# Two of eight tiles of a LayerNorm moved from VectorE to GpSimd and ScalarE, in a two-layer decoder step

## What is computed

```python
def layer_norm(x, g, b):
    xc = x - jnp.mean(x, -1, keepdims=True)
    var = jnp.mean(xc * xc, -1, keepdims=True)
    return xc * lax.rsqrt(var + LN_EPS) * g + b

for l in range(2):
    h = layer_norm(ALPHA * h + 0.5 * swiglu(h, ...), ln_g[l, 0], ln_b[l, 0])   # norms 0 and 3
    m = ab_mixer(h, ...) if l == 0 else gdn_mixer(h, ...)                      # RWKV-7 and retention; gated DeltaNet
    h = layer_norm(ALPHA * h + m, ln_g[l, 1], ln_b[l, 1])                      # norms 1 and 4
    h = layer_norm(ALPHA * h + 0.5 * swiglu(h, ...), ln_g[l, 2], ln_b[l, 2])   # norms 2 and 5
```

## Time and profile before

| | us |
|---|---|
| median of three runs | 1461.27 |
| lowest, highest run | 1460.04, 1465.32 |
| the profiled execution, whole | 1460.42 |
| its span, first to last instruction | 1458.6 |
| TensorE busy in it | 1393.0 (95%) |
| VectorE, ScalarE, GpSimd busy | 895.3 (61%), 648.1 (44%), 456.6 (31%) |

### The profile page before, as it was taken

How to read it: one execution, slowest core, us unless ns; L and a number is a source line. 1 busy time by engine, 2 the same in 40 slices (tenths; PEclk the granted TensorE clock), 3 DMA queues, 4 the chain that set the end, 5 groups by cost and what they waited for, 6 DMA issues and landing times.

```text
span 1458.6 us, 30569 instructions
## 1 busy us (share of the span) xinstructions
PE 1393.0 (95%) x12058; PEld 1325.9 (91%) x12058; DVE 895.3 (61%) x1194; ACT 648.1 (44%) x990; POOL 456.6 (31%) x478
## 2 busy tenths in 40 slices
PE   7999999887999999999999999999998899999996
PEld 7999999776979799999999999988987778999996
DVE  4444456776564565554677775568777467565554
ACT  4333336634234354333444443377683445333333
POOL 3333133542324212125312127431017551221343
PEclk9999999999999999999999999999999999999999
DMA  7555543310333355555445555434433125555541
GB/s 286 159 164 177 179 143 103 102 46 21 110 101 131 110 166 162 168 169 179 143 131 163 168 169 179 143 96 145 129 115 144 31 79 182 161 169 159 182 159 53
DMA packets 50767, 203.39 MB, mean 139 GB/s; under 512 B 5712, under 2 KB 5840, under 8 KB 49904
## 3 DMA queue, kind: packets, MB, share of 16 engines
q1 hardware_dynamic: 46368, 181.03, 38.8%
q0 software_dynamic: 4016, 19.81, 3.7%
q10 hardware_dynamic: 288, 1.18, 0.2%
HBM read 192.17 MB, written 9.83 MB: 138 GB/s over the span
## 4 chain that ended last, share of the span: by engine, by line
PE 83%; DVE 8%; ACT 4%; issue 3%; POOL 1%; DMA 0%; ACTq 0%; POOLq 0%; DVEq 0%
PE gemm L2661 23%; PE gemm L2665 23%; PE gemm L2662 23%; ACT whi L2593 2%; DVE wlo L2598 2%; DVE r L3114 1%; PE job L1790 1%; DVE rstd L3080 1%; PE job L892 1%; PE job L1729 0%; PE job L566 0%; PE job L2670 0%; POOL xsum L3212 0%; PE job L910 0%; DVE M L2323 0%
## 5 line engine op out<-in xcount | busy, mean ns | idle before, releaser
L2661 PE MATMUL gemm<-xhi,whi 128*128 128x290 f32 (+1 forms) x2032 | 615.0, 303 | 21.5 <-DVE wlo L2598 18.6
L2593 ACT ACTIVATE whi<-raw 128x1024 fp32r<-128x1024 f32 (+1 forms) x319 | 358.4, 1124 | 600.2 <-PE gemm L2665 596.5
L2598 DVE TENSOR_TENSOR wlo<-raw,whi 128x1024 fp32r<-128x1024 f32 (+1 forms) x319 | 433.7, 1360 | 301.9 <-ACT whi L2593 299.4
L2665 PE MATMUL gemm<-xlo,whi 128*128 128x290 f32 (+1 forms) x2032 | 606.5, 298 | 3.4 <-DVE xlo L3120 1.6
L2662 PE MATMUL gemm<-xhi,wlo 128*128 128x290 f32 (+1 forms) x2032 | 603.1, 297 | 0.0
L2661 PEld LDWEIGHTS gemm<-xhi,whi 128*128 128x128 f32 x2032 | 385.0, 189 | 35.4 <-DVE wlo L2598 21.2
L2665 PEld LDWEIGHTS gemm<-xlo,whi 128*128 128x128 f32 x2032 | 385.1, 190 | 5.8 <-DVE xlo L3120 2.3
L2662 PEld LDWEIGHTS gemm<-xhi,wlo 128*128 128x128 f32 x2032 | 385.8, 190 | 1.7
L2661 PE MATMUL gemm<-hhi,whi 128*128 128x288 f32 x704 | 209.7, 298 | 2.6 <-POOL hlo L3228 1.9
L2662 PE MATMUL gemm<-hhi,wlo 128*128 128x288 f32 x704 | 210.3, 299 | 0.0
L2665 PE MATMUL gemm<-hlo,whi 128*128 128x288 f32 x704 | 209.2, 297 | 0.0
(11 more groups left out here) (451 smaller groups left out, 1476.5 us busy)
## 6 DMA issues: line engine op xcount, KB each, us to landing
raw<-in_w_dram SPq DMA_DIRECT2D x255, 512.0 KB, 3.5
raw<-in_w_dram SPq DMA_DIRECT2D x64, 704.0 KB, 4.1
M<-in_ret_in_dram POOLq DMA_DIRECT2D x1, 2048.0 KB, 12.6
out_ret_s_dram<-M POOLq DMA_DIRECT2D x1, 2048.0 KB, 8.1
s_space<-in_gdn_in_dram POOLq DMA_DIRECT2D x4, 512.0 KB, 5.8
M<-in_gdn_in_dram POOLq DMA_DIRECT2D x4, 512.0 KB, 5.8
out_gdn_s_dram<-s_space POOLq DMA_DIRECT2D x4, 512.0 KB, 5.0
out_gdn_s_dram<-M POOLq DMA_DIRECT2D x4, 512.0 KB, 6.7
```

The costliest lines, as they stand in the source:

```text
L2593: nc.scalar.activation(whi[c % SPL][:, 0:w], raw[c % RAW][:, 0:w], ACT.Copy).then_inc(hi_ready, 1)
L2598: nc.vector.tensor_tensor(wlo[c % SPL][:, 0:w], raw[c % RAW][:, 0:w], whi[c % SPL][:, 0:w].bitcast(F32), ALU.subtract).then_inc(lo_ready, 1)
L2661: pe.matmul(bank[:, 0:w_], whi[s][:, w], hi[:, f0 + q, 0:w_], start=first, stop=False)
L2665: mm = pe.matmul(bank[:, 0:w_], whi[s][:, w], lo[:, f0 + q, 0:w_], start=False, stop=last)
```

## The change

VectorE scales tiles 0 to 5 and forms their low parts; tiles 6 and 7 are taken from it. GpSimd multiplies these two by rstd in place (`scale_tiles`), in norm 0 behind `a_mu1` and ahead of the wait for `shift_in`, in norm 3 behind the clearing of columns and ahead of the wait for `conv_in`, in norm 5 right behind `sum_tiles`. ScalarE applies ln_g as scale and ln_b as bias for the two, writes xhi and x of tile 6, xhi and x of tile 7, and then x of tiles 0 to 5. GpSimd forms their low parts as x - xhi (`low_tiles`), behind the copies `shift_pad` and `conv_pad`. A new semaphore, `pool_tiles`, counts GpSimd's four steps of a norm (two in norm 5): ScalarE waits for the first two, TensorE (`low_part_in`) for the others; the counts of `scaled` and `x_lo` are adapted.

```diff
--- before.py
+++ after.py
@@ -402,6 +402,20 @@
                 eng.wait_ge(sem("early"), (DT - 1) * EARLY[n] + d + 1)
             else:
                 eng.wait_ge(bank_free[2], TABLE[NORM_STAGE[n]][3][2] + DT // 2)
+
+        def lows_before(version):
+
+            return DT // 2 * version - sum(X_VERSION[n] < version for n in (0, 3))
+
+        def tiles_done(n):
+            return (0, 3, 5).index(n)
+
+        def low_part_in(pe, version, q):
+            for n in (0, 3):
+                if X_VERSION[n] == version and q >= DT - 2:
+                    pe.wait_ge(sem("pool_tiles"), 4 * tiles_done(n) + q - DT + 5)
+                    return
+            pe.wait_ge(x_lo[q % 2], lows_before(version) + q // 2 + 1)
 
         def wait_count(eng, s, count):
             if not isinstance(count, int) or count > 0:
@@ -1486,9 +1500,11 @@
             at = PCOLS["mu"][0]
             pool.wait_ge(sem("const_in"), 64)
             G.tensor_scalar(a_mu1, par[:, at:at + ZA], -1.0, 1.0, ALU.mult, ALU.add)
+            env["scale_tiles"](0)
             pool.wait_ge(sem("shift_in"), 16)
             G.tensor_copy(a_zp[:, :, 1 + SEQ:ZPW].rearrange("p t (b s) -> p t b s", s=5)[:, :, :, 0], a_sh
                           ).then_inc(sem("shift_pad"), 1)
+            env["low_tiles"](0)
 
             at = PCOLS["ka"][0]
             link(G.tensor_scalar(a_km, par[:, at:at + 4], 1.0, None, ALU.subtract))
@@ -2408,9 +2424,11 @@
             stage_read(pool, "down2")
             pool.dma_start(g_cin, a["conv_in"]).then_inc(sem("conv_in"), 16)
             G.memset(g_raw[:, :, 0:3], 0.0)
+            env["scale_tiles"](3)
             pool.wait_ge(sem("conv_in"), 16)
             G.tensor_copy(g_raw[:, :, 3 + SEQ:PADW].rearrange("p k (b s) -> p k b s", s=7)[:, :, :, 0:3],
                           g_cin).then_inc(sem("conv_pad"), 1)
+            env["low_tiles"](3)
             pool.wait_ge(sem("soft"), 1)
             link(G.tensor_scalar(rows_g, rows_g, 0.0, None, ALU.max))
             link(G.tensor_tensor(rows_g, rows_g, rows_e, ALU.add))
@@ -2620,7 +2638,7 @@
                     pe.wait_ge(x_hi, DT * version + q + 1)
                     pe.matmul(gemm[j][:, 0:T], whi[s][:, w], xhi[:, q, :], start=q == 0, stop=False)
                     pe.matmul(gemm[j][:, 0:T], wlo[s][:, w], xhi[:, q, :], start=False, stop=False)
-                    pe.wait_ge(x_lo[q % 2], DT // 2 * version + q // 2 + 1)
+                    low_part_in(pe, version, q)
                     pe.matmul(gemm[j][:, 0:T], whi[s][:, w], xlo[:, q, :], start=False, stop=False)
 
             def stage(name, version, behind=None, late=None, begun=0):
@@ -2899,17 +2917,29 @@
                                      bias=eps).then_inc(drained[bank_of(("var", n))], 1)
 
             def finish_norm(n):
+                done, final = tiles_done(n), f"norm{n}" == phases[-1]
+
+                def new_tile(d):
+                    gain = 1.0 if d < DT - 2 else pc("ln_g", n * DT + d)
+                    nc.scalar.activation(x[:, d, :], r3[:, d, :], ACT.Identity, bias=pc("ln_b", n * DT + d), scale=gain
+                                         ).then_inc(sem("x_new"), 1)
+
                 for d in range(DT):
-                    act.wait_ge(sem("scaled"), DT * (n - sum(k < n for k in LATE_SCALE)) + d + 1)
-                    b = pc("ln_b", n * DT + d)
-                    if f"norm{n}" != phases[-1]:
-                        nc.scalar.activation(xhi[:, d, :], r3[:, d, :], ACT.Identity, bias=b).then_inc(x_hi, 1)
+                    if d < DT - 2:
+                        act.wait_ge(sem("scaled"), (DT - 2) * done + d + 1)
                     else:
-                        nc.scalar.activation(x[:, d, :], r3[:, d, :], ACT.Identity, bias=b).then_inc(sem("x_new"), 1)
-                if f"norm{n}" != phases[-1]:
-                    for d in range(DT):
-                        nc.scalar.activation(x[:, d, :], r3[:, d, :], ACT.Identity, bias=pc("ln_b", n * DT + d)
-                                             ).then_inc(sem("x_new"), 1)
+                        act.wait_ge(sem("pool_tiles"), 4 * done + d - DT + 3)
+                    if final:
+                        new_tile(d)
+                        continue
+                    gain = 1.0 if d < DT - 2 else pc("ln_g", n * DT + d)
+                    nc.scalar.activation(xhi[:, d, :], r3[:, d, :], ACT.Identity, bias=pc("ln_b", n * DT + d), scale=gain
+                                         ).then_inc(x_hi, 1)
+                    if d >= DT - 2:
+                        new_tile(d)
+                if not final:
+                    for d in range(DT - 2):
+                        new_tile(d)
 
             for q in range(2):
                 act.dma_start(x[:, 4 * q:4 * q + 4, :], a["x"][:, 4 * q:4 * q + 4, :]).then_inc(sem(f"x_in{q}"), 16)
@@ -3214,6 +3244,22 @@
                         link(ins)
                 ins.then_inc(sem("summed"), 1)
 
+            def scale_tiles(n):
+                done = tiles_done(n)
+                pool.wait_ge(sem("scaled"), (DT - 2) * done + 1)
+                pool.wait_ge(sem("rest_taken"), 6 * done + 6)
+                for d in range(DT - 2, DT):
+                    nc.gpsimd.tensor_tensor(r3[:, d, :], r3[:, d, :], rstd[:, 0:T], ALU.mult
+                                            ).then_inc(sem("pool_tiles"), 1)
+
+            def low_tiles(n):
+                done = tiles_done(n)
+                for d in range(DT - 2, DT):
+                    pool.wait_ge(x_hi, DT * X_VERSION[n] + d + 1)
+                    pool.wait_ge(sem("x_new"), DT * done + d - DT + 3)
+                    nc.gpsimd.tensor_tensor(xlo[:, d, :], x[:, d, :], xhi[:, d, :].bitcast(F32), ALU.subtract
+                                            ).then_inc(sem("pool_tiles"), 1)
+
             def split_hidden(ffn):
                 use = TABLE[f"up{ffn}"][3]
 
@@ -3241,7 +3287,7 @@
                     nc.gpsimd.tensor_scalar(x[:, d, :], x[:, d, :], pc("ln_g", n * DT + d), pc("ln_b", n * DT + d),
                                             ALU.mult, ALU.add).then_inc(sem("x_late"), 1)
 
-            env = dict(link=link)
+            env = dict(link=link, scale_tiles=scale_tiles, low_tiles=low_tiles)
             low_parts(pool, nc.gpsimd, 0, 1, lambda d: x[:, d, :])
 
             pool.dma_start(cst[:], a["const"]).then_inc(sem("const_in"), 16)
@@ -3258,6 +3304,8 @@
                         late_x(n)
                 elif kind == "norm":
                     sum_tiles(n)
+                    if n == 5:
+                        scale_tiles(n)
                     if n == 4:
                         for h in range(4):
                             for y in range(2):
```

## The result

| us | before | after |
|---|---|---|
| median, nine runs each | 1465.32 | 1468.91 |
| lowest to highest | 1458.95 to 1467.71 | 1465.47 to 1473.47 |
| profiled execution (span) | 1460.42 (1458.6) | 1470.01 (1468.2) |

The ratio of after to before is 1.0039 with the 95% interval [1.0024, 1.0054], some 5.7 us (the two medians lie 3.6 us apart): slower, though within the 0.5% that the prediction called the same. The forecast was 1464.5, its range ended at 1467.5, and 1468.91 lies above it. Before's nine runs hold the three of the prediction; their median, 1465.32, lies 4 us above the 1461.27 that the forecast stood on.

The account below looks back on a forecast made before the run. TensorE, busy 1393.0 of 1458.6 us, was taken to bound the kernel. Norms 0, 3 and 5 added 1.0 + 1.1 + 1.1 = 3.2 us to the median 1461.27, giving 1464.5; range 1459.8 to 1467.5.

Parts of the forecast that it names:

- the dear bound: All three norms: VectorE waits out GpSimd's longest row, 1.03 us, for each of two operations; 2.06 us a norm, 6.2 in all.
- Norm 5, 1.1: End of kernel: scalings 3 to 5 lose 1.1 us, so ScalarE's tiles 5 to 7 and the last store come later.
- Turns of 0.55 us: All three norms: VectorE and GpSimd alternate, each GpSimd operation between two of VectorE's costing VectorE 0.55 us.
- Norm 3, 1.1: Second mixer's norm: two multiplications among scalings 3 to 5 delay the sixth, ScalarE's train and TensorE by 1.1 us.
- some 1 us later: Norms 0 and 3: GpSimd's copies shift_pad and conv_pad come about 1 us later, long before the mixers' first consumers.
- ScalarE's form, nothing (-0.1 to +0.1): ScalarE, tiles 6 and 7: a weight as scale costs nothing extra, judged by L2891's 531 ns against some 0.54 in L2906.
- Norm 0, 1.0: First mixer's norm: delayed scalings and low-part collisions put TensorE's last low-part matmul at 240.09 instead of 239.05, +1.0 us.
- Rival 3: Norm 3: a clock fall on top, 3.4 us at 1.2 GHz, worth 1.7 us of work; 1466.2 us, chance 0.10.
- Rival 1: All norms: no collision between GpSimd's multiplications and VectorE; gain 0.2 us, in norm 0; 1461.1 us, chance 0.13.
- rival 2: All norms: real relief, VectorE leading ScalarE to its last tile; each norm 0.86 us earlier, 2.6 in all; 1458.7, chance 0.03.
- The Trainium skill's rule: VectorE with two SBUF inputs and GpSimd reading SBUF exclude each other for whole instructions; 1.62 us instead of 1.1 per norm.
- the milder price of the rows: Earlier trace's pairs of VectorE and GpSimd operations: 0.55 us per GpSimd operation, as the waiting operation's start overlaps the other.

Follow-up runs that it names:

- e8: Changed kernel, with VectorE copying the inverse deviation to PSUM and its six scalings reading it there; one run, 1464.15 us.
- e3: Changed kernel, with ScalarE's scale for tiles 6 and 7 set to the constant 1.0, their weight left out; one run, 1469.83 us.
- e7: Changed kernel, with six filler matmuls behind the single unit of norm 3, in TensorE's pause; 1468.53 us in 7 runs, ratio to before 1.0030.
- e10: The same kernel as e5, timed in twelve runs: 1468.66 us, ratio to before 1.0034.
- e1: Changed kernel, with GpSimd's multiplications of norms 0 and 3 right behind its mean-taking, ahead of the load's issue; one run, 1469.81 us.
- e5: Changed kernel, with GpSimd waiting for its short operation to complete before it multiplies in norms 0 and 3; one run, 1462.41 us.
- e6: Changed kernel, with the load's issue (shift_in, conv_in) moved behind GpSimd's two multiplications; one run, 1471.18 us.
- e9: Kernel before, with the inverse deviation written to PSUM and the eight scalings reading it there; 1461.96 us, ratio to before 0.9993.
- e11: e9 with norm 3's eight copies of x made by GpSimd behind the low parts instead of by ScalarE; 1458.47 us, ratio to before 0.9960.

## Why the prediction missed

The sign was right, and so was the view that scalings taken from the end of VectorE's row give nothing where ScalarE's train sets the end (e8). The time missed by 1468.91 - 1464.5 = 4.4 us. Read from the traces, this has two parts.

**The base.** The sum was put on the median of three runs, 1461.27. Beside the experiments before ran 40 more times, with a mean of 1463.7 us, which is also that of the nine. That is 2.4 us of the miss. The range put nothing on this term: its top was the same median plus the dear bound, though one of the three runs, 1465.32, lay 4 us higher.

**The sum.** Forecast 1.0 + 1.1 + 1.1 = 3.2; TensorE's program shows 1.2 + 2.7 + 1.1 = 5.0. That is another 1.8 us, nearly all of it in norm 3.

- *Norm 5, 1.1*: measured 1.08. Turns of 0.55 us, as the earlier trace rows said. ScalarE's weights cost 0.18 more on its train, which the end did not show.
- *Norm 3, 1.1*: measured 2.70. The sixth scaling came 2.34 us later instead of 1.1. The step that failed is "each GpSimd operation that falls between two of VectorE's costs VectorE 0.55 us": the earlier trace rows show GpSimd with no issue in front, while both loads are issued directly ahead of `scale_tiles`. The dear bound, 2.06 us per norm, lay nearer: the stall cost 2.36 - 0.51 = 1.85 us in norm 3 and 2.10 - 0.51 = 1.59 in norm 0. The other 0.48 us is the copy into `conv_pad`, which was to come "some 1 us later" at no cost. It came to lie on a scaling. Before, it fell on a low part, off ScalarE's path:

```profile
965.15 1.00 DVE L3120 SCALAR_TENSOR_TENSOR xlo<-r,par,xhi 128x288 fp32r<-128x288 f32 x1
...
964.92 0.96 POOL L2412 COPY M<-M 128x576 f32<-128x576 f32 x1 [2.25 <-DMA M<-in_conv_in_dram]
```

- *ScalarE's form, nothing (-0.1 to +0.1)*: 0.61 instead of 0.52 us, 0.36 us in norms 0 and 3 (e3). L2891 of the earlier trace rows has a scale from a column of `par` but no bias, so it stood for one column; the new form reads two. The groups by line of before have one with a bias alone and one, a square, with no column:

```profile
L2911 ACT ACTIVATE x<-r,par 128x288 f32<-128x288 f32 x16 | 7.0, 521 | 0.0
L2893 ACT ACTIVATE x<-r 128x288 f32<-128x288 f32 x16 | 6.8, 427 | 0.0
```

  So 427 ns without a column, 521 to 531 with one, 0.61 us with two: each adds some 0.09, as far as a square may be compared. With 2.34 + 0.36 = 2.70 the norm adds up.
- *Norm 0, 1.0*: measured 1.2, in part by luck. GpSimd's two subtractions were to fall among VectorE's low parts, for 2 x 0.55 us; they began at +7.04, behind the start of the last of these at +6.99, so that this term fell away, while the stall put the sixth scaling 1.57 us later instead of 1.1. The stall and the weights moved ScalarE's train by 1.91 us (+10.12 instead of +8.21), but here it stood beside TensorE's own first unit, and only 1.2 reached the path. The forecast had the train only 1.1 later, in step with TensorE.

**The rivals.** Rival 3, a clock fall on top, is what after's trace shows behind norm 3, and one more behind norm 0; it had a chance of 0.10, and its time, 1466.2, stood on the same low base. How much of the total is clock can be judged from all runs together, as each has a time and a mean granted clock. Before's four runs at 0.993 took 1459.2 to 1459.9 us, those at 0.990 and 0.991 1460.3 to 1463.2, those at 0.987 1465.0 to 1468.0. With one level for each kernel, a run is 1.14 (+-0.08, here and below the 95% interval) us longer for each 0.001 of clock. After's nine runs have a mean of 0.9871, before's forty of 0.9891, so 2.3 us; at equal clock after is 3.6 (+-0.6) us slower. By the same working e10 is 2.9 (+-0.6) us slower than before. Two things stay open. Why the clock falls more often in after is not settled: e7 had one fall less and others instead, and e10, with shorter pauses, had the same mean, 0.9874. And the 3.6 us at equal clock are less than the 5.0 read from TensorE's program: by this reading the 3.2 of the forecast lies inside the interval, and the miss is base and clock. It puts the difference of after and e10, the stall and what follows from it, at 0.7 (+-0.7) us, where the traces show 5.0 - 3.5 = 1.5. So the stall is shown in the traces; the timed runs alone do not settle what it is worth. Rival 1 fell with the 2.10 and 2.36 us, rival 2 with ScalarE's last copy, at +10.86 instead of +8.15 in norm 3.

The Trainium skill's rule (SBUF — State Buffer, "Who interferes with whom"), taken by the letter, would have put the forecast 1.5 us higher. Norm 5, e1, e5 and e6 speak for the milder price of the rows, norms 0 and 3 of after, with 1.59 and 1.85 us, lie at and above the rule's 1.62.

## What to carry to other kernels

Price a moved operation by rows that show the same neighbours on its new engine, not only the same operation: what stood right in front of it (a load's issue, no completion wait) raised VectorE's wait for two operations from 1.1 to 1.59 and 1.85 us. Before work is moved off an engine, follow back who sets the end of that place; here ScalarE did, so scalings taken from the end of VectorE's row gave nothing in norm 3 (e8), while first scalings that end earlier (e9) and eight copies taken from ScalarE (e11) did. With differences below 1%, take a median of many runs as the base and read each run's granted clock before a change is blamed or praised: one run of e5 took 1462.4 us, the median of twelve was 1468.7.

## What the hardware showed that was not expected

- A VectorE operation waited out two GpSimd operations in a row, 2.10 and 2.36 us instead of 0.51, behind a load issued by GpSimd; with that issue behind them the same two cost 1.06 and 1.06 us.
- With one of VectorE's two operands in PSUM there is no wait on either side: 0.51 us beside GpSimd's 0.80. The first two scalings of the three norms, 0.61 and 1.06 us in norm 0 of before, also fall to 0.51.
- ScalarE's activation on 128 x 288 takes 0.43, 0.52 and 0.61 us with no, one and two operands read from a column (the first of these a square).
- The kernel before took 1458.95 to 1468.0 us in 49 runs, and in the forty beside the experiments most of the scatter goes with the mean granted clock, 0.993 down to 0.986. In the profiled executions the clock is at one of its two levels, and what differs is how often and how long it falls.
